# Stick-breaking attention by pairs of heads, with a mask matmul and a two-pass fp32r cumulation, in a two-block kernel

## What is computed

```python
def block(args):                       # 128 queries against all keys
    strict = key_pos[None, :] < q_pos[:, None]
    z = jnp.einsum('bthd,bshd->bhts', qb, k) * (HEAD_DIM_2 ** -0.5)
    brk = jnp.where(strict, jax.nn.softplus(z), 0.0)
    later = jnp.pad(brk[..., 1:], ((0, 0), (0, 0), (0, 0), (0, 1)))
    remain = lax.cumsum(later, axis=3, reverse=True)
    log_a = jax.nn.log_sigmoid(z) - remain
    a = jnp.where(strict, jnp.exp(log_a), 0.0)
    o = jnp.einsum('bhts,bshd->bthd', a, v)
```

## Time and profile before

| | us |
|---|---|
| median of 3 runs | 1354.71 |
| lowest and highest | 1353.22 and 1357.62 |
| the profiled execution | 1361.22 |
| its span in the profile | 1359.5 |
| PE busy | 1253.9 (92%) |
| DVE busy | 794.2 (58%) |
| ACT busy | 613.7 (45%) |
| POOL busy | 107.8 (8%) |
| PE's share of the chain that ended last | 75% |

### The profile page before, as it was taken

How to read it: one execution, slowest core, us unless ns; L and a number is a source line. 1 busy time by engine, 2 the same in 40 slices (tenths; PEclk the granted TensorE clock), 3 DMA queues, 4 the chain that set the end, 5 groups by cost and what they waited for, 6 DMA issues and landing times.

```text
span 1359.5 us, 20850 instructions
## 1 busy us (share of the span) xinstructions
PE 1253.9 (92%) x8513; PEld 1146.1 (84%) x8513; DVE 794.2 (58%) x1257; ACT 613.7 (45%) x950; POOL 107.8 (8%) x172
## 2 busy tenths in 40 slices
PE   1799999898979899999989598999999999899998
PEld 1799999876878899887788378999989987899997
DVE  6786998654486354455446746555555433665554
ACT  2447623433455454554434335444444554544442
POOL 0100000022030000011100410000000133000000
PEclk9999999997979999999979688999999999899999
DMA  9796789501647556322532044555554321455552
GB/s 321 223 310 200 230 261 312 200 1 34 198 150 226 153 162 204 104 92 94 163 94 70 32 155 131 181 187 187 187 183 149 131 94 62 155 186 186 187 186 93
DMA packets 164879, 219.93 MB, mean 162 GB/s; under 512 B 5868, under 2 KB 135696, under 8 KB 164784
## 3 DMA queue, kind: packets, MB, share of 16 engines
q1 hardware_dynamic: 163984, 216.82, 49.3%
q0 software_dynamic: 800, 1.77, 0.4%
HBM read 217.53 MB, written 1.05 MB: 161 GB/s over the span
## 4 chain that ended last, share of the span: by engine, by line
PE 75%; DVE 11%; DMA 6%; ACT 5%; issue 2%; SPq 0%; DVEq 0%; ACTq 0%
PE ps L636 12%; PE ps L640 11%; PE ps L637 11%; PE ps L693 6%; PE ps L694 6%; PE ps L698 6%; DMA raw_weights<-in_a_w_in 3%; PE ps L666 3%; PE ps L667 3%; DVE w_lo L1543 3%; PE ps L671 3%; DVE acc L1626 2%; ACT w_hi L1223 1%; PE ps L924 1%; DMA raw_weights<-in_kv_w 1%
## 5 line engine op out<-in xcount | busy, mean ns | idle before, releaser
L1543 DVE TENSOR_TENSOR w_lo<-raw_weights,w_hi 128x1024 fp32r<-128x1024 f32 x348 | 423.9, 1229 | 291.4 <-ACT w_hi L1223 289.9
L1223 ACT ACTIVATE w_hi<-raw_weights 128x1024 fp32r<-128x1024 f32 x348 | 362.6, 1054 | 415.3 <-PE ps L698 110.3
L636 PE MATMUL ps<-act_hi,w_hi 128*128 128x256 f32 x1664 | 418.5, 289 | 6.4 <-ACT w_hi L1223 6.4
L637 PE MATMUL ps<-act_lo,w_hi 128*128 128x256 f32 x1664 | 410.1, 284 | 0.0
L636 PEld LDWEIGHTS ps<-act_hi,w_hi 128*128 128x128 f32 x1664 | 320.5, 193 | 14.1 <-issue 10.4
L637 PEld LDWEIGHTS ps<-act_lo,w_hi 128*128 128x128 f32 x1664 | 320.7, 193 | 3.5 <-issue 2.9
L640 PE MATMUL ps<-act_hi,w_lo 128*128 128x256 f32 x1664 | 234.7, 284 | 5.8 <-DVE w_lo L1543 5.8
L640 PEld LDWEIGHTS ps<-act_hi,w_lo 128*128 128x128 f32 x1664 | 215.5, 193 | 6.4 <-DVE w_lo L1543 6.4
L693 PE MATMUL ps<-w_hi,act_hi 128*128 128x512 f32 x360 | 142.7, 396 | 2.3 <-DVE work L1728 1.7
L694 PE MATMUL ps<-w_hi,act_lo 128*128 128x512 f32 x360 | 141.2, 392 | 0.0
L698 PE MATMUL ps<-w_lo,act_hi 128*128 128x512 f32 x360 | 99.2, 389 | 0.0
(11 more groups left out here) (252 smaller groups left out, 1295.6 us busy)
## 6 DMA issues: line engine op xcount, KB each, us to landing
raw_weights<-in_ffn_w SPq DMA_DIRECT2D x66, 1024.0 KB, 5.3
raw_weights<-in_a_w_in SPq DMA_DIRECT2D x32, 1024.0 KB, 6.1
raw_weights<-in_mod_w SPq DMA_DIRECT2D x24, 1024.0 KB, 5.8
raw_weights<-in_kv_w SPq DMA_DIRECT2D x16, 1024.0 KB, 5.8
raw_weights<-in_b_w_in SPq DMA_DIRECT2D x16, 1024.0 KB, 5.4
raw_weights<-in_od_w_qkv SPq DMA_DIRECT2D x12, 1024.0 KB, 5.1
raw_weights<-in_kv_mod_w SPq DMA_DIRECT2D x8, 1024.0 KB, 5.5
raw_weights<-in_a_w_out SPq DMA_DIRECT2D x8, 1024.0 KB, 4.9
```

The lines of the kernel that those rows point to most:

```text
L636: pe.matmul(dst, wh[:, k, :], act_hi[:, base + k, :], start=(k == 0), stop=False)
L637: pe.matmul(dst, wh[:, k, :], act_lo[:, base + k, :], start=False, stop=False)
L1223: act.activation(half_view(w_hi, s), HALVES[s][2], ACT.Copy).then_inc(hi_done, 1)
L1543: dve.tensor_tensor(half_view(w_lo, s), HALVES[s][2], half_view(w_hi, s).bitcast(F32), ALU.subtract).then_inc(lo_done, 1)
```

## The change

- **Pairs.** The loop runs over eight pairs of heads, and four banks (4 to 7) hold scores, two for each pair. The scores (`z_scores`) of the two heads are issued alternately, one on rows 0 to 63 of the array and one on rows 64 to 127. The weighted values alternate between output partitions 0 to 63 and 64 to 127, and go into the heads' own score banks.
- **Order.** In iteration p TensorE does the values of pair p-2, a dense half, the cumulation of pair p-1, the scores of pair p, and a second dense half. VectorE's two copies for pair p-2, its keys copy and its splits up to `last_v + NSPLIT + 2p` come ahead of the softplus steps of pair p. ScalarE reaches that same half after both heads' Ln.
- **Mask.** GpSimd's selects are gone. GpSimd makes a tile `far_r` once, with -1e30 where the key isn't before the query, and TensorE adds it to the scores' diagonal blocks with an identity matmul in fp32r. The softplus of such an entry is 0, and so is its Exp at the end.
- **Cumulation.** VectorE writes the breaks twice, in fp32 (`sb_brk`) and rounded to fp32r (`sb_brk_hi`); GpSimd subtracts them into `sb_brk_lo`, over the first. TensorE makes three fp32r matmuls with each of the two, instead of three in fp32.
- **Constants.** The five constant matrices are an fp32r tile of their own. GpSimd's queue loads the identity and the ones first of all, which SP's queue did before, and the rest in two DMAs instead of one.

The diff, cut to its core:

```diff
         @block.gpsimd
+            pool.dma_start(cst_r[:, 0:256], const[:, 0:256].bitcast(F32R)).then_inc(ident_in, 16)
...
-            pool.dma_start(cst[:, 256:], const[:, 256:]).then_inc(masks_in, 16)
+            pool.dma_start(cst_r[:, 256:], const[:, 256:640].bitcast(F32R)).then_inc(masks_in, 16)
+            pool.dma_start(cst[:, :], const[:, 640:]).then_inc(masks_in, 16)
...
+            pool.tensor_scalar(far_r, causal[:, 0:P], -1.0, FAR, ALU.is_ge, ALU.mult).then_inc(st("sb_far"), 1)
+            for p in range(HO // 2 + 2):
+                if p < HO // 2:
+                    for h in (2 * p, 2 * p + 1):
+                        pool.wait_ge(st("sb_soft"), h + 1)
+                        pool.tensor_tensor(sb_brk_lo[h % 2], sb_brk[h % 2], sb_brk_hi[h % 2].bitcast(F32), ALU.subtract)\
+                            .then_inc(st("sb_lo"), 1)
+                if 1 <= p <= HO // 2:
+                    c = p - 1
                     split_output(c, o_full[:, c % 2, :], st("sb_out"), st("sb_split"), OUT2 + c)
...
+            def z_scores(p):
+                if p % 2 == 0:
+                    wait_read(pe, f"od_q{p // 2}", 0)
+                    wait_read(pe, f"od_k{p // 2}", 0)
+                if p >= 2:
+                    pe.wait_ge(st("sb_out"), p - 1)
+                pair = [(sb_bank(h), slice(HD2 * (h % 2), HD2 * (h % 2) + HD2)) for h in (2 * p, 2 * p + 1)]
+                for bank, _ in pair:
+                    pe.matmul(diagonal_blocks(bank[:, 0:S3]), ident_r,
+                              far_r.rearrange("p (b t) -> p b t", b=1).to_broadcast([P, 2, P]),
+                              start=True, stop=False, skip_group_check=True)
+                for bank, rows in pair:
+                    pe.matmul(bank[:, 0:T], odk[rows, p, 0:P], odq[rows, p, :], start=False, stop=False,
+                              skip_group_check=True)
+                for bank, rows in pair:
+                    ins = pe.matmul(bank[:, T:S3], odk[rows, p, P:T], odq[rows, p, P:T], start=False, stop=False,
+                                    skip_group_check=True)
+                ins.then_inc(st("sb_z"), 1)
...
+            def minus_breaks(p):
+                for h in (2 * p, 2 * p + 1):
+                    bank = sb_bank(h)
+                    pe.wait_ge(st("sb_lo"), h + 1)
+                    for b in (sb_brk_hi[h % 2], sb_brk_lo[h % 2]):
+                        pe.matmul(bank[:, 0:T], neg_after_r, b[:, 0:T], start=False, stop=False, skip_group_check=True)
+                        pe.matmul(bank[:, P:T], neg_ones_r, b[:, T:S3], start=False, stop=False, skip_group_check=True)
+                        ins = pe.matmul(bank[:, T:S3], neg_after_r, b[:, T:S3], start=False,
+                                        stop=(b is sb_brk_lo[h % 2]), skip_group_check=True)
+                    ins.then_inc(st("sb_log"), 1)
...
+            for p in range(HO // 2 + 2):
+                if p >= 2:
+                    weighted_values(p - 2)
+                dense_half(2 * p)
+                if 1 <= p <= HO // 2:
+                    minus_breaks(p - 1)
+                if p < HO // 2:
+                    z_scores(p)
+                dense_half(2 * p + 1)
...
-            sp.dma_start(cst[:, 0:256], const[:, 0:256]).then_inc(ident_in, 16)
...
+            for p in range(HO // 2 + 2):
+                if p >= 2:
+                    c = p - 2
+                    dve.wait_ge(st("sb_o"), c + 1)
+                    if c >= 2:
+                        dve.wait_ge(st("sb_split"), c - 1)
+                    dve.tensor_copy(o_full[0:HD2, c % 2, :], sb_bank(2 * c)[0:HD2, 0:T])
+                    dve.tensor_copy(o_full[HD2:P, c % 2, :], sb_bank(2 * c + 1)[HD2:P, 0:T]).then_inc(st("sb_out"), 1)
+                if p < HO // 2:
+                    if p % 2 == 0 and 0 < p <= 6:
+                        take_keys(p // 2)
+                    advance(last_v + NSPLIT + 2 * p)
+                    for h in (2 * p, 2 * p + 1):
+                        e = h % 2
+                        dve.wait_ge(st("sb_ln"), h + 1)
+                        if p >= 1:
+                            dve.wait_ge(st("sb_log"), h - 1)
+                        dve.scalar_tensor_tensor(out=sb_brk[e], in0=sb_bank(h)[:, 0:S3], scalar=0.0, in1=sb_ln_t[e],
+                                                 op0=ALU.max, op1=ALU.add)
+                        dve.scalar_tensor_tensor(out=sb_brk_hi[e], in0=sb_bank(h)[:, 0:S3], scalar=0.0, in1=sb_ln_t[e],
+                                                 op0=ALU.max, op1=ALU.add).then_inc(st("sb_soft"), 1)
```

More of the change, by code:

```diff
@@ L150, in build @@
         f_pick = sb("f_pick", [48, HA], F32R)
+        with nc.sbuf_tensor("big_rounded", [P, 5 * ARRAY], F32R) as big_r:
+            pass
         big = sb("big", [P, 5, ARRAY])
@@ L158, in build @@
         small = sb("small", [P, 256])
+        with nc.sbuf_tensor("work_rounded", [P, 3584], F32R) as work_r:
+            pass
         work = sb("work", [P, 3584])
[L161 to L165, removed]
+        ident_r, ones_r, ones64_r, neg_after_r, neg_ones_r = (cst_r[:, n * P:(n + 1) * P] for n in range(5))
+        ident, ones = ident_r.bitcast(F32), ones_r.bitcast(F32)
+        ones64, neg_after, neg_ones = ones64_r.bitcast(F32), neg_after_r.bitcast(F32), neg_ones_r.bitcast(F32)
+        causal = cst[:, 0:384]
+        chunk_go = cst[:, 384:640]
+        inv_count = cst[:, 640:704].rearrange("p (g t) -> p g t", g=4)
         def grid(n, heads=HA):
@@ L553, in _ @@
                 split_output(c, o_full[:, c % 2, :], st("ds_out"), st("ds_split"), OUT2 + c)
[L555 to L568, removed]
+            pool.wait_ge(st("ds_split"), HE // 2)
+            pool.tensor_scalar(far_r, causal[:, 0:P], -1.0, FAR, ALU.is_ge, ALU.mult).then_inc(st("sb_far"), 1)
[7 more added lines that the diff above has]
+                    c = p - 1
                     split_output(c, o_full[:, c % 2, :], st("sb_out"), st("sb_split"), OUT2 + c)
@@ L1117, in _ @@
                 project_tokens("od_v", "od_in", SELF)
[L1119 to L1131, removed]
@@ L1145, in weighted_values @@
+            def weighted_values(p):
+                pe.wait_ge(st("sb_exp"), 2 * p + 2)
+                if p == 0:
                     wait_read(pe, "od_v", 3)
                     wait_read(pe, "od_v", 2)
[L1147 to L1163, removed]
+                heads = [(h, sb_bank(h)[HD2 * (h % 2):HD2 * (h % 2) + HD2, :], sb_prob[h % 2])
+                         for h in (2 * p, 2 * p + 1)]
@@ L1164, in _, with dense_half @@
+                for h, bank, pr in heads:
+                    pe.matmul(bank[:, 0:T], odv[:, 0, h * HD2:(h + 1) * HD2], pr[:, 0:T], start=True, stop=False)
+                for h, bank, pr in heads:
+                    ins = pe.matmul(bank[:, P:T], odv[:, 1, h * HD2:(h + 1) * HD2], pr[:, T:S3], start=False, stop=True)
+                ins.then_inc(st("sb_o"), 1)
+            def dense_half(i):
                 if i < 12:
+                    s = next_half("od_in")
                     if i % 2 == 0:
-                        bank = open_unit(f"od_{'qk'[i // 2 % 2]}{1 + i // 4}")
```

98 lines of the change are left out of this document (41 added, 57 removed).

## The result

The changed kernel is slower by a little: 1364.49 us against 1354.03 for the kernel before on the same chip, a ratio of 1.0068 (95% interval 1.0042 to 1.0095), so +9.2 us. In a second series on another chip it was 1.0038 (1.0009 to 1.0068), +5.2. The forecast of +7.5 lies between; with intervals of some 4 us either way, so close a match is in part luck.

What follows compares the result with a forecast made beforehand. TensorE bounds the stage before the change, the loop through the four engines after it, at 10.7 us a pair. Stage +5.8, clock +2.1 and start -0.4 give +7.5 on a median of 1354.71: 1362.2 us, range 1356 to 1370.

Steps and rivals of the forecast that it cites:

- TensorE's share of a pair: TensorE's own work for two heads in the stick-breaking stage: 9.35 us against 11.18 before.
- The loop: Path through ScalarE, VectorE, GpSimd and TensorE from one pair's first Abs to the next: 10.7 us, the new bound.
- The keys: VectorE's late keys copies: 1.2 us each in iterations 2 and 4, a 16.0 us period in iteration 6.
- The first period: Time between the first two pairs' first Abs, taken as 10.7 us like other undisturbed periods.
- rival 2: GpSimd's first-head subtraction shut out until VectorE's four steps end, or clock worse: +6.3 us, 1368.5; chance 0.1.
- The clock: TensorE's granted clock falls after the 6.8 us wait in iteration 6: +2.1 us, with 0 as other end.
- The gaps of the other pairs: TensorE waits of about 1.3 us in pairs outside iteration 6, priced at nothing for the clock.
- The start: One DMA fewer on SP's queue ahead of the weights at kernel start: -0.4 us, at worst 0.
- The cover: Identity lands by about 6.1 us, ready at 6.6 before VectorE's first weights at 6.98; gone above 5.7 us.
- The sum: Whole kernel: stage +5.8, clock +2.1, start -0.4, total +7.5 us.
- The rival of halves that don't overlap: A pair's scores take 1.5 us instead of 0.9 on TensorE: +4.2 more, 1366.4; chance 0.13.
- That TensorE stays the bound: Rival: loop under 9.35 us and keys copy not late, seven periods of 9.35, 1343.0; chance 0.08.

Runs made afterwards that it cites:

- the kernel with both edits: Changed kernel with VectorE's keys copies and second low split both moved behind the pair's four softplus steps: 1341.35 us (0.9877) and 1342.94 us (0.9918) against the kernel before.
- both edits with GpSimd twice: The kernel with both edits, with each of GpSimd's subtractions done twice, the first result unused: ratio 0.9977 to the kernel before.

## Why the prediction was right

- **TensorE's share of a pair**, 9.35 us: the kernel with both edits, where TensorE is the bound, has 9.38. Its parts: cumulating 0.64 to 0.68 a head (0.68), mask 0.37 (0.34), scores 0.86 (0.9 taken, 0.64 and 1.5 as ends), values 0.80 from 1153.93 to 1154.73 (0.75). A single head's scores take 0.84 to 0.85, so 0.86 for a pair is the halves overlapping in full; the end of 0.64 had left out the time to the next kind of matmul.
- **The loop**, 10.7: 10.43 in the undisturbed iterations. Its places are where they were forecast: VectorE's idle time up to ScalarE's split (5.1 to 5.6 us in six of the pairs, 7.1 in pair 1 and 11.1 in pair 6, 49.8 in all), the second subtraction's end at 8.4 (8.45), TensorE's waits for GpSimd (6.1 us in eight places). From there to the next pair's first Abs it took 2.0, not 2.25: the second head's cumulating 0.74 (0.85), scores and handing over 0.97 (1.1).
- **The keys**: iterations 2 and 4 cost 1.14 and 1.24 more (1.2). Iteration 6 is 17.21, with 1.4 of it the clock, so 15.8 (16.0), and the wait 6.47 (6.8).
- **The first period** was missed: 11.39 instead of 10.7. In iteration 0 no copies stand between VectorE's steps and its next low split. That split starts at 1065.79, just ahead of the second subtraction, and this one takes 1.95. The forecast had only the split wait for GpSimd, not the other way round; its rival 2 came near, but with the first head's subtraction.
- **The clock**: 2.1 taken, 1.4 found. TensorE was at full clock again after some 3 us of work, where 4.2 had been taken. The gaps of the other pairs, priced at nothing, cost nothing in the first profile and 3.5 us in the second: right about one execution and wrong about the next. This is the term that was mis-sized, in either direction, and that the forecast held in the first profile is luck as far as this term goes.
- **The start**: -0.4. TensorE has the last small vector at 13.45 instead of 13.84. But the identity came at 6.83, not 6.1, and VectorE's first step slipped from 6.98 to 7.32. The cover was gone, as the prediction named; it cost nothing because VectorE caught up before that vector was needed.
- **The sum**: stage and clock +7.9 forecast, +6.0 and +9.5 in two profiles. The 1.9 missing in the first are errors that partly cancel: +0.7 in the first period, -0.9 in the long one, -1.4 in the other five, and -0.4 up to the first Abs. The rival of halves that don't overlap falls with 0.86 and 0.80. That TensorE stays the bound needed what the forecast said, a loop under 9.4 and an earlier copy; the kernel with both edits has the two. Its 1341 to 1343 fit the 1343.0 of that rival, and its stage is 13.0 shorter than before, where the rival's terms give 11.3.

## What to carry to other kernels

When a change shortens the busiest engine's work, count the loop through the other engines first: here a saving of 1.8 us a pair was lost, most of it to one low split that stood ahead of the steps TensorE waits for, the rest to a late copy. In an engine's queue, work that waits for a third engine belongs behind the steps of the loop, and a copy that frees a bank belongs as soon as its unit is done. Then ask again what each new operation is worth: its sign can depend on that order.

## What the runs showed of the hardware

- The pair's fp32 matmuls on two row halves of the array took 0.86 us where one head took 0.84 to 0.85, and those on two column halves 0.80 where one took 0.79. Both overlap in full, and for the rows the order in which they are issued did not matter (0.87).
- VectorE's low split and GpSimd's subtraction, both with two inputs in SBUF, hold each other up, and the later one pays. A split that begins inside a subtraction takes 1.31 to 1.66 us instead of 1.23, and 2.09 where nearly the whole subtraction was still to come (1153.73, both edits with GpSimd twice). A subtraction that begins just after a split takes 1.95 instead of 1.01. The Trainium skill ("SBUF — State Buffer", "Who interferes with whom") states this lock and that the order of issue decides which side is blocked; the trace agrees on both.
- The granted clock can fall or stay with the same gaps of about 1 us, from one execution to the next, and a fall lasted over 6 us.
